# The first feed-forward network: two pairs of row blocks per group as seven products instead of four pairs, their sums of weights moved from GpSimd to VectorE

## The reference, cut to what matters

```
hn = rmsnorm(h, ffn_norm)                                       # [256, 2048]
h  = h + (silu(hn @ w_gate) * (hn @ w_up)) @ w_down             # w_gate, w_up: [2048, 5632]
```

## Time and profile before

| | |
|---|---|
| median of 3 runs | 2385.93 us (2385.33 to 2386.66) |
| the profiled execution's own time | 2385.7 us |
| its span, first to last instruction | 2383.9 us |
| instructions | 28969 |
| TensorE busy | 2334.9 us, 98% |
| VectorE busy | 1703.5 us, 71% |
| ScalarE busy | 1249.1 us, 52% |
| GpSimd busy | 324.0 us, 14% |

### The profile page before, as it was taken

The page is one execution under the profiler, slowest core; times in us unless marked ns, Lnnn a source line. Parts: engine busy times, 40 slices in busy tenths (PEclk is TensorE's granted clock), DMA queues, the critical chain, the costliest instruction groups (busy, mean ns, idle before and its releaser), DMA issues.

```text
span 2383.9 us, 28969 instructions
## 1 busy us (share of the span) xinstructions
PE 2334.9 (98%) x11166; PEld 1935.3 (81%) x11166; DVE 1703.5 (71%) x2235; ACT 1249.1 (52%) x1837; POOL 324.0 (14%) x167
## 2 busy tenths in 40 slices
PE   8999999999899999999999999999999999999998
PEld 7888888888777777777888887778888888888886
DVE  6445565666899999998565666667888888885444
ACT  6445454545555555555454566656444444444442
POOL 1000000000556566562000100000000000000000
PEclk9999999999999999999999999999999999999999
DMA  7665555656555655555656665445666666666664
GB/s 259 186 190 170 159 172 153 188 185 187 185 177 177 198 184 183 190 188 173 211 185 194 189 206 165 146 142 178 192 188 191 189 192 188 192 188 194 193 194 151
DMA packets 226425, 439.28 MB, mean 184 GB/s; under 512 B 13632, under 2 KB 17888, under 8 KB 225904
## 3 DMA queue, kind: packets, MB, share of 16 engines
q1 hardware_dynamic: 224400, 429.51, 58.6%
q0 software_dynamic: 1888, 7.93, 1.1%
HBM read 435.24 MB, written 2.15 MB: 183 GB/s over the span
## 4 chain that ended last, share of the span: by engine, by line
PE 87%; DVE 9%; ACT 2%; issue 1%; POOL 1%; DMA 0%; DVEq 0%; ACTq 0%; POOLq 0%
PE bank L1652 19%; PE bank L1654 19%; PE bank L1653 19%; PE bank L1683 14%; PE bank L1685 7%; DVE wlo L1097 6%; DVE WX L1097 2%; PE bank L1695 2%; PE bank L1631 1%; PE bank L1633 1%; PE bank L1632 1%; ACT whi L772 1%; PE bank L1839 1%; PE bank L1860 1%; PE bank L1738 0%
## 5 line engine op out<-in xcount | busy, mean ns | idle before, releaser
L1097 DVE TENSOR_TENSOR wlo<-raw,whi 128x1024 fp32r<-128x1024 f32 (+3 forms) x717 | 883.6, 1235 | 610.6 <-ACT whi L772 608.8
L772 ACT CAST whi<-raw 128x1024 fp32r<-128x1024 f32 (+3 forms) x717 | 734.4, 1026 | 898.2 <-PE bank L1654 630.0
L1683 PE MATMUL bank<-TT,whi 128*128 128x512 f32 x1408 | 488.9, 394 | 0.8 <-DVE TT L1345 0.7
L1652 PE MATMUL bank<-whi,TT 128*128 128x512 f32 (+1 forms) x1048 | 421.5, 402 | 9.5 <-DVE wlo L1097 7.6
L1654 PE MATMUL bank<-whi,TT 128*128 128x512 f32 (+1 forms) x1048 | 407.8, 389 | 0.0
L1653 PE MATMUL bank<-wlo,TT 128*128 128x512 f32 (+1 forms) x1048 | 407.2, 389 | 0.0
L1685 PE MATMUL bank<-TT,wlo 128*128 128x256 f32 x1408 | 390.1, 277 | 0.0
L1683 PEld LDWEIGHTS bank<-TT,whi 128*128 128x128 f32 x1408 | 264.0, 188 | 62.5 <-issue 1.3
L1685 PEld LDWEIGHTS bank<-TT,wlo 128*128 128x128 f32 x1408 | 264.2, 188 | 0.0
L1652 PEld LDWEIGHTS bank<-whi,TT 128*128 128x128 f32 x1048 | 197.5, 188 | 55.9 <-DVE wlo L1097 15.0
L1654 PEld LDWEIGHTS bank<-whi,TT 128*128 128x128 f32 x1048 | 197.5, 188 | 41.1
(11 more groups left out here) (279 smaller groups left out, 3488.3 us busy)
## 6 DMA issues: line engine op xcount, KB each, us to landing
raw<-in_ffn_w_up_dram SPq DMA_DIRECT2D x176, 512.0 KB, 3.6
raw<-in_w_in_dram SPq DMA_DIRECT2D x120, 512.0 KB, 3.7
raw<-in_w_down_dram SPq DMA_DIRECT2D x88, 512.0 KB, 4.6
raw<-in_ffn_w_down_dram SPq DMA_DIRECT2D x88, 512.0 KB, 4.7
raw<-in_w_gate_dram SPq DMA_DIRECT2D x58, 512.0 KB, 3.8
raw<-in_w_up_dram SPq DMA_DIRECT2D x58, 512.0 KB, 4.5
raw<-in_swa_w_in_dram SPq DMA_DIRECT2D x48, 512.0 KB, 3.7
raw<-in_w_out_dram SPq DMA_DIRECT2D x32, 512.0 KB, 4.6
```

The costliest lines, as they stand in the source:

```text
L772: eng.copy(hi_at(u)[:, 0:src.shape[-1]], src).then_inc(s_cast, 1)
L1097: eng.tensor_tensor(lo_at(u)[:, 0:n], src, hi_at(u)[:, 0:n].bitcast(F32), ALU.subtract).then_inc(s_lo, 1)
L1652: eng.matmul(o, lh[:, ts], hi[:, kk, :], start=start, stop=False)
L1683: eng.matmul(o[:, :], hi[:, kk, fs], TT[:, k, :, :].rearrange("p a s -> p (a s)"), start=k == 0, stop=False)
```

## The change

`SUMS` is now the first two pairs (0, 1); the other six are plain (`PLAIN`). A group is 12 x 12 + 2 x 21 = 186 matmuls in 19 steps, each 1024 wide: six plain gate chunks, six plain up chunks and seven steps of sums, in this order, written g0..g5, u0..u5 for the plain ones and a, b for the two pairs:

g0 g1 C(a) C(b) g2 D B(a) B(b) g3 E g4 A g5 u0 u1 u2 u3 u4 u5

C and B are 6 matmuls for one pair; D, E and A hold one kind of product for both pairs, 6 matmuls each. Instead of four extra banks, four kinds of product (C, B, E, A) go one after the other through the up group's second bank; behind each kind ScalarE copies the bank out (`snap`, 128 x 512, into `ST`), and TensorE's next kind, or u0 after the last, waits for that copy (`s_snap`). Each copy stands behind the cast that its place in ScalarE's queue gives it: after C(b) at g2, after B(b) at g3, after E at g4, after A at g5.

VectorE forms the sums of weights: per pair one subtraction of 1024 columns (`add0`) and two of 512, each using the one before (`add1`). They stand at u2 (add0 a), u3 (add1 a), u4 (add0 b) and the next group's g1 (add1 b); for the first group at g0 and g1. GpSimd has nothing left in this stage but one small `row_rstd`. The four `sum` additions now read `ST` only; two stand at g5, two at u1. The product with silu (formerly a step `hid` of its own) now follows the emptying of the up banks directly, at the next g0, second half first.

The pairs a and b have four `raw` slots of their own; the plain chunks share the slots 4, 5 and 6 in turn (`RX` has three now). The fetches of the next group's a and b stand between those of u2 and u3 and between those of u4 and u5.

The diff, cut to its core:

```diff
-SUMS = (1, 2, 3, 4)
-ORDER0, ORDER = (0, 1, 5, 2, 3, 4), (1, 0, 2, 5, 3, 4)
+SUMS = (0, 1)
+PLAIN = (2, 3, 4, 5, 6, 7)
...
     for f in range(NF):
-        paired(("gate", f, "w_gate", 512 * f), ("up", f, "w_up", 512 * f), ORDER if f else ORDER0, (6, 7))
+        ahead = sums(f + 1) if f < NF - 1 else []
+        turn = [("gate", f, p) for p in PLAIN] + [("up", f, p) for p in PLAIN]
+        if f == 0:
+            turn = turn[:2] + sums(0) + turn[2:]
+        for z in turn[:-3] + ahead[:2] + turn[-3:-1] + ahead[2:] + turn[-1:]:
+            network(*z)
...
+        gate = [("w", at["gate", f, p]) for p in PLAIN]
+        a, b = (at["gate", f, p] for p in SUMS)
+        rows += gate[:2] + [("C", a), ("C", b), gate[2], ("D", a), ("B", a), ("B", b), gate[3], ("E", a), gate[4],
+                            ("A", a)] + gate[5:]
+        rows += [("w", at["up", f, p]) for p in PLAIN]
...
         if FFN <= t < DN:
-            z = (min((0, 2, 4), key=lambda x: used.get(x, x - 100)) if (t - FFN) % 2 == 0 else slot[-1] + 1)
+            p = chunks[t][2] // 2
+            if p in SUMS:
+                z = 2 * SUMS.index(p) + (chunks[t][0] == "up")
+            else:
+                z = min((4, 5, 6), key=lambda x: used.get(x, x - 100))
...
+        for j in range(4):
+            put(g[2 + j], "snap", 4 * f + j)
         if f:
+            for b in range(2):
+                put(g[2 + b], "htr", 2 * f - 2 + b)
+                put(g[3 + b], "hsp", 2 * f - 2 + b)
+        put(u[1], "silu", f)
+        put(g[5], "sum", 2 * f)
+        put(u[1], "sum", 2 * f + 1)
         if f < NF - 1:
-            put(tail + 3, "sq", f + 1)
+            for c in range(2):
+                put(u[2 + 2 * c], "add0", 2 * f + 2 + c)
+                put(u[3] if c == 0 else num["gate", f + 1, PLAIN[1]], "add1", 2 * f + 2 + c)
...
-            for n, t in enumerate(cells):
-                if n == 1:
-                    row_rstd(3)
-                sums(n, t)
+            row_rstd(3)
...
+                elif name == "snap":
+                    f, j = divmod(i, 4)
+                    a, b = (num["gate", f, p] for p in SUMS)
+                    ac.wait_ge(s_mm, step_of[(("C", b), ("B", b), ("E", a), ("A", a))[j]] + 1)
...
+                    copy(ST[:, j, :], bank[banks["up", f][1]][:, :]).then_inc(s_snap, 1)
...
+                elif name in ("add0", "add1"):
+                    f, c = divmod(i, 2)
+                    z = raw[:, 2 * c:2 * c + 2, :].rearrange("p c (k n) -> p (c k) n", k=2)
+                    if name == "add0":
+                        for st in ("gate", "up"):
+                            n = num[st, f, SUMS[c]]
+                            ve.wait_ge(l_raw[rslot[n]], 16 * raw_load[n])
+                        if f:
+                            ve.wait_ge(s_lo, step_of["A", first_sums[f - 1]] + 1)
+                        eng.tensor_tensor(TS[:, c, 0:2, :], z[:, 2:4, :], z[:, 0:3:2, :], ALU.subtract).then_inc(s_add, 1)
+                    else:
+                        ve.wait_ge(s_add, 3 * i + 1)
+                        eng.tensor_tensor(TS[:, c, 2, :], z[:, 3, :], TS[:, c, 0, :], ALU.subtract).then_inc(s_add, 1)
+                        ve.wait_ge(s_add, 3 * i + 2)
+                        eng.tensor_tensor(TS[:, c, 3, :], z[:, 1, :], TS[:, c, 2, :], ALU.subtract).then_inc(s_add, 1)
...
                 if kind == "C":
-                    products = ((main(gate, 0), rows(even, 0)), (temporary(0), rows(odd, 0)))
+                    products = ((up, 1, rows(2 * one, 0)), (gate, 0, rows(2 * one + 1, 0)))
...
+                elif kind == "E":
+                    pe.wait_ge(s_snap, 4 * f + 2)
+                    products = tuple((up, 1, sums_of_rows(p, 3)) for p in pairs)
                 else:
-                    products = ((main(("up", f), 0), sums_of_rows(4)),)
+                    pe.wait_ge(s_snap, 4 * f + 3)
+                    products = tuple((up, 1, sums_of_rows(p, 1)) for p in pairs)
...
                 pe.wait_ge(s_lo, u + 1)
+                if st == "up":
+                    pe.wait_ge(s_snap, 4 * i + 4)
```

More of the change, by code:

```diff
@@ L68, in weight_chunks, with network, sums @@
     nf = [(512 * i, 512) for i in range(NF)]
[L70 to L77, removed]
-    for f in range(NF):
-        paired(("gate", f, "w_gate", 512 * f), ("up", f, "w_up", 512 * f), ORDER if f else ORDER0, (6, 7))
-    for h in range(2):
-        paired(*[("dn", i, "w_down", 512 * i) for i in (2 * h, 2 * h + 1)], range(18), range(18, 22))
+    def network(st, f, p):
+        rows.append((st, f, 2 * p, 2, 512, "w_" + st, 512 * f))
+    def sums(f):
+        return [(st, f, p) for p in SUMS for st in ("gate", "up")]
+    for f in range(NF):
+        ahead = sums(f + 1) if f < NF - 1 else []
[4 more added lines that the diff above has]
+            network(*z)
+    for h in range(2):
+        for p in range(18):
+            for i in (2 * h, 2 * h + 1):
+                rows.append(("dn", i, 2 * p, 2, 512, "w_down", 512 * i))
+        for i in (2 * h, 2 * h + 1):
+            for p in range(18, 22):
+                rows.append(("dn", i, 2 * p, 2, 512, "w_down", 512 * i))
     product("in2", "swa_w_in_2", [(2048, 512), n4[0], (2560, 512)] + n4[1:], KT)
@@ L94, in weight_chunks, with network_chunks @@
     return rows
+def network_chunks(chunks):
+    return {(row[0], row[1], row[2] // 2): t for t, row in enumerate(chunks) if row[0] in ("gate", "up")}
 def weight_steps(chunks):
[L103 to L111, removed]
+    at = network_chunks(chunks)
+    rows = [("w", t) for t in range(FFN)]
+    for f in range(NF):
+        gate = [("w", at["gate", f, p]) for p in PLAIN]
[3 more added lines that the diff above has]
+        rows += [("w", at["up", f, p]) for p in PLAIN]
+    return rows + [("w", t) for t in range(DN, END)]
 def ring_slots(work):
@@ L167, in groups_of @@
     for g in sorted(before, key=lambda z: last[z]):
-        for half in range(2):
+        for half in (1, 0) if g[0] == "up" else (0, 1):
             by = "V" if g[0] == "in2" and g[1] in (0, 2) else EMPTIED_BY[g[0]][half]
@@ L244, in side_steps @@
         put(t + 1, "rs", 3 + v)
+    num = network_chunks(chunks)
     for f in range(NF):
-        tail = FFN + 16 * f + 12
+        g, u = ([num[st, f, p] for p in PLAIN] for st in ("gate", "up"))
         if f == 0:
[L248 to L251, removed]
-        if f:
[L253 to L258, removed]
+            for c in range(2):
+                put(g[c], "add0", c)
+                put(g[c], "add1", c)
+        for j in range(4):
+            put(g[2 + j], "snap", 4 * f + j)
+        if f:
+            for b in range(2):
[4 more added lines that the diff above has]
+        put(u[1], "sum", 2 * f + 1)
         if f < NF - 1:
-            put(tail + 3, "sq", f + 1)
+            for c in range(2):
+                put(u[2 + 2 * c], "add0", 2 * f + 2 + c)
+                put(u[3] if c == 0 else num["gate", f + 1, PLAIN[1]], "add1", 2 * f + 2 + c)
     for b in range(2):
@@ L531, in build @@
         first, last, order, banks, bank_before, emptied = groups_of(chunks)
-        steps = side_steps()
+        steps = side_steps(chunks)
+        assert not any(steps[t] for t in range(END) if t not in stands.values())
+        num = network_chunks(chunks)
+        first_sums = [num["gate", f, SUMS[0]] for f in range(NF)]
         side_bank, side_before, side_last = side_banks(steps)
@@ L1632, in stream_sums @@
+                for b, (g, half, (lh, ll)) in enumerate(products):
+                    fresh = begins(g, half)
+                    if (g, half) == (up, 1):
+                        fresh = (kind in "CB" and one == SUMS[0]) or (kind in "EA" and b == 0)
+                    o = bank[banks[g][half]]
+                    eng.matmul(o[:, :], lh, hi[:, b, :], start=fresh, stop=False)
                     eng.matmul(o[:, :], lh, lo[:, b, :], start=False, stop=False)
-                    mm = eng.matmul(o[:, :], ll, hi[:, b, :], start=False, stop=stop)
+                    read = (kind in "CB" and one == SUMS[1] and b == 0) or (kind in "EA" and b == 1)
+                    mm = eng.matmul(o[:, :], ll, hi[:, b, :], start=False, stop=read)
```

195 lines of the change are left out of this document (85 added, 110 removed).

## The result

The changed kernel takes 2357.48 us in the median of 4 runs (2357.37 to 2358.41), the kernel before 2385.8 beside it: a ratio of 0.9882, 95% interval 0.9865 to 0.9899. That is 28.3 us, 1.2% faster; the forecast was 2362.4. In a later set of runs the changed kernel took 2357.93, ratio 0.9886 (0.987 to 0.9903).

The account below looks back on a forecast made before the run. The prediction took VectorE, with GpSimd beside it, as the bound, costing TensorE about 45 us. Ten periods fall from 450.0 to 434.4 us and the rest from 53.45 to 45.6: 23.5 less, 2362.4 us, range 2355 to 2376.

Parts of the forecast that it names:

- The bound: First feed-forward network: TensorE waits about 45 us of 503.45, held by VectorE with GpSimd beside it.
- the pace: TensorE's true time where it never waits, read in the next stage: 0.2267 us a matmul, 2.72 us a chunk.
- The added 15.0 us of matmuls: TensorE, first feed-forward network: six matmuls a group more, 66 in all, with nothing to hide them.
- floor: TensorE's time for a group's matmuls and transposes without waits: 43.04 us after the change, 1.96 under today's 45.0.
- VectorE's sum: VectorE's work per group after the change: 34.0 us of 43.0, or 35.4 with `add0` at its upper bound.
- The walk: Step-by-step timing of one group, g0 to 43.04 us: low parts, copies and fetches in time, copy margins 1.1 to 2.9.
- the allowance for waits: TensorE's waits after the change: 0.4 us a group, from nothing to 1.5, and 2.5 us in the first group.
- the step I had named: First group, B(a): its low part ready at 14.5 us and due at 13.0, a wait of 1.5 us.
- VectorE still comes late: Rival: VectorE's bunches at the group's turn make TensorE wait 1.5 us a group, 2374.5 us; chance 0.20.
- One bank: Rival: copies of the shared bank two casts later expose three, 2.6 us a group, about 2385; chance 0.05.
- u2 lands late: Rival: u2's fetch at 7.3 us delays the fourth copy, 3.1 us a group, 2392 us; chance 0.07.

Follow-up runs that it names:

- all_plain: The kernel before with no pair as seven products (`SUMS` empty): 16 plain chunks, 192 matmuls a group, no sums; 2375.8 us, ratio 0.996.
- new_gpsimd: The changed kernel with the two pairs' sums of weights (`add0`, `add1`) moved back from VectorE to GpSimd; 2382.9 us, ratio 0.9988.
- new_noise: The changed kernel, sums still on VectorE, with GpSimd given useless additions, two behind each plain step; 2410.1 us, ratio 1.010.
- three_vector_best: The kernel before with three pairs, sums on VectorE and one step earlier in its queue, first group beginning with two gate chunks; 2356.1 us, ratio 0.9878.
- two_gpsimd_old: The kernel before with only the number of pairs changed, four to two, GpSimd still making the sums; 2361.1 us, ratio 0.990.

## Why the prediction was right, point by point

**The bound, and the pace.** The reading that the stage lost 45 us to TensorE's waits held: the changed kernel lost 2.1. It rests on the start times. The page's digits hardly carry it: where GpSimd works, one slice of TensorE's has an 8 and the others the 9 that they have elsewhere. The added 15.0 us of matmuls were paid; `all_plain`, with as many matmuls more again, has a group of 44.7 us against a floor of 44.4. The other stages did not move: from the stage's end to the last instruction it is 1273.3 us after (2355.6 - 1082.27) and 1273.8 before.

**VectorE's sum.** Forecast 34.0 us a group, measured 33.7 over nine groups. `add0` at the price of a subtraction: 1218 ns.

**The walk.** One group, with C(b)'s end (forecast 8.16) at 702.55, so g0 at 694.4; ScalarE's timeline:

```profile
702.55 1.06 ACT L783 CAST whi<-TS 128x1024 fp32r<-128x1024 f32 x1 [0.30 <-PE bank L1664]
...
718.99 1.05 ACT L783 CAST whi<-RX 128x1024 fp32r<-128x1024 f32 x1 [0.82 <-DMA RX<-in_w_up_dram]
719.94 0.59 ACT L756 ACTIVATE ST<-bank 128x512 f32<-128x512 f32 x1
...
729.55 1.05 ACT L783 CAST WX<-RX 128x1024 fp32r<-128x1024 f32 x1 [2.06 <-DMA RX<-in_w_up_dram]
```

u2 was fetched at 715.18, 20.8 us in (forecast 20.9), and its cast began at 24.6 (24.5); the fourth copy ended at 720.53, 26.1 (26.15), 0.4 us before u0's first matmul at 720.94; u5's cast began at 35.15 (34.3 plus). Next g2's low part was ready at 743.67 us, 49.3 (48.7), due at 51.2. Every step lies within 1 us of the walk, and ScalarE did wait for fetches by up to 2.5 us, as the walk allows, without TensorE's noticing:

```profile
742.45 1.22 DVE L1114 TENSOR_TENSOR wlo<-RX,whi 128x1024 fp32r<-128x1024 f32 x1
```

**The term that was off.** It is the allowance for waits, 0.4 us a group and 2.5 us in the first, 6.5 in all, where 2.1 were lost. By the transposes a group took 43.13 us, 0.1 over the floor of 43.04 and not 0.4; ten such periods are 431.3 us, forecast 434.4. Outside them stand 475.6 - 431.3 = 44.3 us, forecast 45.6: the first group lost 1.2 us. Its one wait was 0.9 us for B's low part, the step I had named, at 1.5. The pace of 0.2267 us a matmul was right. The shorter 42.93 by the gate's emptying does not contradict it: that is the short last period again. Together 27.8 for 23.5.

**The rivals.** *VectorE still comes late* happened only in that one wait of 0.9 us; with GpSimd put back beside it, in `new_gpsimd` and `new_noise`, it is what TensorE waits for in every group or nearly. *One bank* and *u2 lands late* did not happen, but both mechanisms are shown to be real, with their size. Without cover two copies cost 2.1 us a group, some 1.05 each where the walk priced one at 1.64; the rule of the Trainium skill (Perfetto Trace Analysis, "Matmuls"), that independent groups of matmuls should rotate through banks, describes that run, and the plain steps between the kinds are what buys it off. With one slot less TensorE waits for exactly the fourth copy, and the kernel is slower than before. The margin of the changed kernel there is thin: in the ten groups after the first the fourth copy ends 0.4 to 0.8 us before u0 starts, where the walk had 0.6. In its trace a fetch takes 4.1 us in the median and 8.5 at most from issue to landing, but u2's 3.8 or less: in the group walked through above the fetch before it was issued 4.4 us earlier, at 710.82.

**What the prediction had wrong though its time came out.** It took GpSimd's slowing of VectorE and the late sums as the thing that the change takes away, and counted the whole gain to it. The runs give another account. From the kernel before, halving the pairs alone takes 44.9 us of loss to 3.9 for 15 us of matmuls, 24 us of gain, with GpSimd still at work. The new order and the new maker together add 3.6, which the two overlapping intervals leave open (the stage is 1.7 us shorter in the traces), and they hang together: the new order with GpSimd is at 2382.9, VectorE with the old order at 2365.6, both worse than neither. VectorE's load does not decide alone either: at 86% with GpSimd the loss is 19.4 us, at 90% without it 9.7. The time came out all the same because the sum is the floor plus what the walk leaves, and in neither does it matter which of the edits freed VectorE.

**Open.** Why two pairs on VectorE lose 4.2 us more in the old order than on GpSimd is traced only in part: by the transposes a group takes 43.45 us against 43.22, which is half of it, and the other 2.2 us lie before the second group's transposes. That the sums stand in front of A's subtraction is the likely cause for the groups, not shown: one step earlier took 0.2 us a group in the kernel with three pairs. New order with three pairs was not tried: its `TS` and `EX` would leave no room for the third slots.

## What to carry to other kernels

A trick that saves TensorE work and adds work to a feeding engine has a best number of uses, and it can lie at half of what fits: vary the number alone, and count a saving only up to where TensorE begins to wait. The feeder's busy share does not say where that is. VectorE at 90% cost TensorE 0.2 us a group over the floor in `three_vector_best`, and at 88% it cost 4.9 in `new_noise`; what decides is how late it comes at the turn of the group. Before crediting the move of an operation to another engine, run the smaller edit that the change also contains.

Where a shared buffer is copied out, what counts is the step that lies between, and which slow thing stands in the copying engine's queue ahead of the copy.

## What the runs showed of the hardware

The slowing by GpSimd is not a share but a collision of single instructions. An operation of VectorE that reads two operands in SBUF and starts while one of GpSimd runs ends its own time after GpSimd's end: the addition of 734.68 us ends at 737.50, 0.56 us after GpSimd's of 734.54; that of 741.99 ends 0.54 after GpSimd's of 740.85; the subtraction of 1024 columns that starts at 725.09 ends 1.08 after GpSimd's of 722.78. How much it costs depends only on when it starts, so 0.68 us can become 2.9. From 700 to 1060 us all 32 such meetings in `two_gpsimd_old` fit this within 0.02 us, and 36 of 38 in `new_gpsimd`; the other two started within 0.03 us of GpSimd's start, kept their own time, and it was GpSimd's that took longer. So it goes both ways: GpSimd's operation of 2.40 us took 3.48 when it started together with a subtraction (740.85), 1.08 more.

An operation with a PSUM operand keeps its 0.68 us beside the same engine (L1188, L1374). The Trainium skill, GPSIMD Engine Reference, "Key points", names instructions with two SBUF inputs as those that contend; the rows agree.

So nearly the same GpSimd work cost VectorE, per group, 3.5 us in the old order (12.2 us of work; 32.3 busy, against 34.0 with the sums on VectorE less 5.2) and 8.0 in the new one (12.7 us of work; 36.5 against 33.7 less 5.2), of which 5.3 fall on the additions that now read `ST` alone. Copying a bank to SBUF frees the bank, and exposes what reads the copy to GpSimd.
